# A two-block transformer kernel whose residual stream is held with the features on the partitions from the first stage to the last

## What is computed

```python
for n in range(4):
    x = x + 0.5 * swiglu(rms_norm(x, g), w_gate, w_up, w_down)    # d_ff 2816
    x = x + mixer[n](rms_norm(x, g))
    x = x + 0.5 * swiglu(rms_norm(x, g), w_gate, w_up, w_down)
# rms_norm(x, g) = x * rsqrt(mean(x * x, axis=-1) + 1e-6) * g
# swiglu(h, wg, wu, wd) = (silu(h @ wg) * (h @ wu)) @ wd
```

## Time and profile before

| | us |
|---|---|
| median of 3 runs | 2869.38 (2861.89 to 2871.81) |
| span of the profiled execution, first to last instruction | 2865.5 |
| TensorE busy | 2586.2 (90%) |
| VectorE busy | 1564.4 (55%) |
| ScalarE busy | 1133.1 (40%) |
| GpSimd busy | 88.5 (3%) |
| moved by DMA | 409.58 MB, 143 GB/s on average |

### The profile page before, as it was taken

How to read it: one execution, slowest core, us unless ns; L and a number is a source line. 1 busy time by engine, 2 the same in 40 slices (tenths; PEclk the granted TensorE clock), 3 DMA queues, 4 the chain that set the end, 5 groups by cost and what they waited for, 6 DMA issues and landing times.

```text
span 2865.5 us, 41213 instructions
## 1 busy us (share of the span) xinstructions
PE 2586.2 (90%) x17302; PEld 2356.7 (82%) x17302; DVE 1564.4 (55%) x1965; ACT 1133.1 (40%) x1254; POOL 88.5 (3%) x85
## 2 busy tenths in 40 slices
PE   5999977999999668999999888799999998887999
PEld 4998965899998547998999876689989897675898
DVE  3555664555555775455555644655555555456544
ACT  3333443433434244334334552343333345433432
POOL 2000000000000203000000000030000000000000
PEclk9999977999999779999999987999999999889999
DMA  5554521455455304554554422255545544222454
GB/s 167 187 190 133 177 74 33 158 190 179 160 190 162 115 0 106 189 190 157 181 189 151 135 90 69 89 164 188 186 154 189 167 150 130 85 89 74 162 184 138
DMA packets 306697, 409.58 MB, mean 143 GB/s; under 512 B 9367, under 2 KB 272861, under 8 KB 306589
## 3 DMA queue, kind: packets, MB, share of 16 engines
q1 hardware_dynamic: 303360, 400.61, 43.5%
q0 software_dynamic: 2496, 5.49, 1.1%
q10 hardware_dynamic: 732, 1.98, 0.2%
HBM read 407.00 MB, written 1.05 MB: 142 GB/s over the span
## 4 chain that ended last, share of the span: by engine, by line
PE 79%; DVE 12%; ACT 6%; issue 2%; DMA 1%; DVEq 0%; ACTq 0%; SPq 0%
PE bank L458 35%; PE acc L466 21%; PE bank L781 13%; ACT parts L393 3%; PE bank L723 2%; DVE parts L400 2%; PE bank L777 2%; PE bank L852 1%; DMA raw<-in_ffn_w_up 1%; PE bank L1721 1%; PE bank L871 1%; PE bank L639 1%; PE bank L1599 1%; DVE x L560 1%; DVE stat L613 1%
## 5 line engine op out<-in xcount | busy, mean ns | idle before, releaser
L400 DVE TENSOR_TENSOR parts<-raw,parts 128x2048 fp32r<-128x2048 f32 x383 | 877.9, 2292 | 927.1 <-ACT parts L393 923.3
L393 ACT ACTIVATE parts<-raw 128x2048 fp32r<-128x2048 f32 x383 | 730.6, 1908 | 1297.2 <-PE bank L458 630.4
L458 PEld LDWEIGHTS bank<-hT,parts 128*128 128x128 f32 x8448 | 1024.4, 192 | 9.2 <-DVE parts L400 2.5
L458 PE MATMUL bank<-hT,parts 128*128 128x256 f32 x8448 | 1028.2, 283 | 2.1 <-DVE parts L400 2.1
L466 PE MATMUL acc<-parts,gated 128*128 128x512 f32 x2400 | 564.8, 392 | 12.3 <-DVE gated L707 7.4
L466 PEld LDWEIGHTS acc<-parts,gated 128*128 128x128 f32 x2400 | 447.9, 189 | 104.3 <-issue 8.7
L781 PE MATMUL bank<-parts,hT 128*128 128x256 f32 (+2 forms) x3504 | 438.1, 288 | 15.3 <-DVE parts L400 9.9
L781 PEld LDWEIGHTS bank<-parts,hT 128*128 128x128 f32 x3504 | 433.3, 197 | 22.1 <-DVE parts L400 14.5
L528 DVE TENSOR_TENSOR silu_gate<-bank,silu_gate 128x512 f32<-128x512 f32 x88 | 60.9, 691 | 138.9 <-PE bank L458 138.9
L723 PE MATMUL bank<-squares,x 128*128 128x128 f32 x384 | 76.7, 380 | 58.7 <-DVE squares L752 52.9
L723 PEld LDWEIGHTS bank<-squares,x 128*128 128x128 f32 x384 | 71.4, 286 | 66.6 <-DVE squares L752 57.8
(11 more groups left out here) (342 smaller groups left out, 1528.9 us busy)
## 6 DMA issues: line engine op xcount, KB each, us to landing
raw<-in_ffn_w SPq DMA_DIRECT2D x132, 1024.0 KB, 5.2
raw<-in_w_in SPq DMA_DIRECT2D x52, 1024.0 KB, 5.3
raw<-in_ffn_w_gate SPq DMA_DIRECT2D x44, 1024.0 KB, 5.3
raw<-in_ffn_w_up SPq DMA_DIRECT2D x44, 1024.0 KB, 5.3
raw<-in_ffn_w_down SPq DMA_DIRECT2D x44, 1024.0 KB, 4.8
raw<-in_hy_w_in SPq DMA_DIRECT2D x22, 1024.0 KB, 5.3
raw<-in_hy_w_out SPq DMA_DIRECT2D x8, 1024.0 KB, 4.8
raw<-in_w_out SPq DMA_DIRECT2D x8, 1024.0 KB, 4.9
```

The costliest lines, as they stand in the source:

```text
L393: t.e.activation(parts[:, n % PARTS, 0, 0:size], raw[:, n % RAW, 0:size], ACT.Copy).then_inc(hi_ready, 1)
L400: t.e.tensor_tensor(parts[:, n % PARTS, 1, 0:size], raw[:, n % RAW, 0:size], parts[:, n % PARTS, 0, 0:size].bitcast(F32), ALU.subtract).th ...
L458: mm = pe.matmul(bank[:, up_bank(t, c, which), f * S:(f + 1) * S], slot_cols(s, w)[:, k, f * P:(f + 1) * P], hT[:, h, k, :], start=(k == 0 ...
```

## The change

The residual is kept as `xT`, eight tiles of 128 features by 256 tokens.

- Down and output products (`down_tile`, L486 of the new file) have the weights stationary and 256 tokens streaming: 48 matmuls of 256 columns for a piece in place of 24 of 512. Their sums come out with the features on the partitions, two feature tiles to a bank of `acc`, one bank after another in the last piece.
- `add_vector` adds each bank to `xT`; `hT` is `xT` times the gain, split, without the root and without a transpose. The squares of `xT` are summed over the eight tiles (`tensor_reduce`, L682); a matmul with a column of ones sums over the partitions (`root_col_tensor`); VectorE makes the root for each token; `root_row_tensor` spreads it over the partitions as `root_row`.
- Since `hT` lacks the root, every product of it is multiplied by the root as it leaves PSUM: token-major results by ScalarE with a scale per partition (two halves, since a half has its own column), feature-major ones by VectorE with `root_row`.
- The gates of the triple mixers and `mix` are feature-major too; their evacuation moves from ScalarE to VectorE, the sigmoid stays on ScalarE and works in SBUF. The transposes of `mix` are gone.
- At the start `x` is transposed once (16 transposes), at the end the result is transposed back and leaves in four transfers.

```diff
-        def down_product(pe, stationary, s, k, a, first, last):
+        def down_tile(pe, rows_hl, moving, d, first, last):
+
             for g, w in PASSES:
-                for n in range(2):
-                    mm = pe.matmul(acc[:, 2 * a + n, :], stationary(g), slot_rows(s, w)[:, k, n * 512:(n + 1) * 512],
-                                   start=(first and g + w == 0), stop=(last and g == 1), skip_group_check=True)
+                mm = pe.matmul(acc[:, d // 2, (d % 2) * S:(d % 2 + 1) * S], rows_hl(w)[:, d * P:(d + 1) * P], moving(g),
+                               start=(first and d % 2 == 0 and g + w == 0), stop=(last and g == 1),
+                               skip_group_check=True)
             return mm
 
-        def ffn_down(pe, c, s, last=False):
-            for a, f in [(a, f) for a in range(TT) for f in range(2)]:
-                mm = down_product(pe, lambda g: gated[:, g, c % 2, f * S + a * P:f * S + (a + 1) * P], s, f, a,
-                                  False, last and f == 1)
-                if last and (a, f) == (0, 1):
+        def ffn_down(pe, c, s, first=False, last=False):
+            for d in range(KD):
+                for f in range(2):
+                    mm = down_tile(pe, lambda w: slot_rows(s, w)[:, f, :],
+                                   lambda g: gated[:, g, c % 2, f * S:(f + 1) * S], d, first and f == 0, last and f == 1)
+                if last and d in (1, 3, 5):
                     mm.then_inc(acc_full, 1)
             mm.then_inc(piece_done, 1)
...
-            for b in range(4):
-                pe.matmul(acc[:, b, :], zeros[:, :], zeros[:, :].unsqueeze(1).to_broadcast([P, 4, P]), start=True,
-                          stop=False, skip_group_check=True)
+            all_taken(t)
             ffn_up(t, 0, arrived(t), 0, hT_waits(t))
-            ffn_up(t, 0, arrived(t), 1)
+            ffn_up(t, 0, arrived(t), 1, between=lambda: root_col_tensor(t))
+            root_row_tensor(t)
...
+                split_hi(t, n + PARTS, i)
+                if c == 0:
+                    t.see(root_col_ready)
+                    root_row_scalar(t)
+                act.wait_ge(gate_scaled, later(CHUNKS * k + c + 1, i, 2))
+                v = silu_gate[:, c % 2, :]
+                act.activation(v, v, ACT.Silu).then_inc(silu_ready, 1)
+                split_hi(t, n + PARTS + 1, i)
...
-                split_lo(t, n + 2, i)
+                if c == 0:
+                    root_col_vector(t)
+                    split_lo(t, n + PARTS)
+                    dve.wait_ge(root_row_ready, t.see(root_row_ready))
+                dve.wait_ge(piece_done, later(PARTS + n + 1, i, LOOP))
+                v = silu_gate[:, c % 2, :]
+                v2 = v.rearrange("p (f s) -> p f s", f=2)
+                dve.tensor_tensor(v2, halves(up_bank(t, c, 0)), root_rows(2), ALU.mult).then_inc(gate_scaled, 1)
+                if c:
+                    split_lo(t, n + PARTS, i)
                 dve.wait_ge(piece_done, later(PARTS + n + 2, i, LOOP))
+                dve.tensor_tensor(up_rows[:, :].rearrange("p (f s) -> p f s", f=2), halves(up_bank(t, c, 1)),
+                                  root_rows(2), ALU.mult).then_inc(gate_made, 1)
+                dve.wait_ge(gate_made, later(3 * (CHUNKS * k + c) + 1, i, 6))
                 dve.wait_ge(silu_ready, later(CHUNKS * k + c + 1, i, 2))
-                v = silu_gate[:, c % 2, :]
-                dve.tensor_tensor(v, bank_of(up_bank(t, c, 1)), v, ALU.mult).then_inc(gate_made, 1)
-                dve.wait_ge(gate_made, later(2 * (CHUNKS * k + c) + 1, i, 4))
+                dve.tensor_tensor(v, up_rows[:, :], v, ALU.mult).then_inc(gate_made, 1)
+                dve.wait_ge(gate_made, later(3 * (CHUNKS * k + c) + 2, i, 6))
                 dve.tensor_copy(gated[:, 0, c % 2, :], v).then_inc(gate_made, 1)
-                dve.wait_ge(gate_made, later(2 * (CHUNKS * k + c) + 2, i, 4))
+                dve.wait_ge(gate_made, later(3 * (CHUNKS * k + c) + 3, i, 6))
                 dve.tensor_tensor(gated[:, 1, c % 2, :], v, gated[:, 0, c % 2, :].bitcast(F32), ALU.subtract)\
                     .then_inc(gated_ready, 1)
-                split_lo(t, n + 3, i)
+                split_lo(t, n + PARTS + 1, i)
...
+        def root_col_tensor(t):
+
+            pe = t.e
+            pe.wait_ge(sums_ready, t.see(sums_ready))
+            for a in range(TT):
+                mm = pe.matmul(acc[:, 0, a:a + 1], sums[:, a * P:(a + 1) * P], one_col[:, :], start=True, stop=True)
+            mm.then_inc(sums_full, 1)
+
+        def root_row_tensor(t):
+
+            pe = t.e
+            pe.wait_ge(root_col_ready, t.see(root_col_ready))
+            for a in range(TT):
+                mm = pe.matmul(acc[:, 1, a * P:(a + 1) * P], root_col[:, a:a + 1].to_broadcast([P, P]), ident,
+                               start=True, stop=True)
+            mm.then_inc(root_row_full, 1)
+            t.roots += 1
+
+        def pre_scalar(t, at):
+
+            act = t.e
+            for b in range(4):
+                act.wait_ge(x_ready, t.see(x_ready))
+                for k in (2 * b, 2 * b + 1):
+                    act.activation(hT[:, 0, k, :], xT[:, k, :], ACT.Copy, scale=gain[:, at + k:at + k + 1])\
+                        .then_inc(hT_hi, 1)
+            act.activation(squares[:, :], xT[:, :, :].rearrange("p k s -> p (k s)"), ACT.Square).then_inc(x_squares, 1)
+            if t.piece:
+                next_hi(t)
...
+        def root_row_scalar(t):
+
+            act = t.e
+            act.wait_ge(root_row_full, t.see(root_row_full))
+            act.activation(root_row[:, :], acc[:, 1, 0:S], ACT.Copy).then_inc(root_row_ready, 1)
+            act.wait_ge(root_row_ready, t.see(root_row_ready))
...
+        def add_vector(t, b, scale):
...
+            acc_filled(t, b, scale is None)
+            v = xT[:, 2 * b:2 * b + 2, :]
+            if scale is None:
+                ins = dve.tensor_copy(v, acc_pair(b))
+            else:
+                ins = dve.scalar_tensor_tensor(v, acc_pair(b), scale, v, ALU.mult, ALU.add)
+            ins.then_inc(x_ready, 1)
...
+        def pre_vector(t, at, scale):
+
+            dve = t.e
+
+            def add(b):
+                add_vector(t, b, scale)
+
+            def low(b):
+                dve.wait_ge(hT_hi, t.see(hT_hi, 2))
+                for k in (2 * b, 2 * b + 1):
+                    dve.scalar_tensor_tensor(hT[:, 1, k, :], xT[:, k, :], gain[:, at + k:at + k + 1],
+                                             hT[:, 0, k, :].bitcast(F32), ALU.mult, ALU.subtract).then_inc(hT_ready, 1)
+
+            add(0)
+            for b in range(1, 4):
+                add(b)
+                low(b - 1)
+            low(3)
+            dve.wait_ge(x_squares, t.see(x_squares))
+            dve.tensor_reduce(sums[:, :], squares[:, :].rearrange("p (k s) -> p s k", k=KD), AX.X, ALU.add)\
+                .then_inc(sums_ready, 1)
+            if t.piece:
+                next_lo(t)
+
+        def root_col_vector(t):
+
+            dve = t.e
+            dve.wait_ge(sums_full, t.see(sums_full))
+            t.link(dve.tensor_copy(stat[:, 0, 0:TT], acc[:, 0, 0:TT]))
+            y, w = root_vector(t, stat[:, 0, 0:TT], D, last_factor=True)
+            dve.tensor_tensor(root_col[:, :], y, w, ALU.mult).then_inc(root_col_ready, 1)
...
-        def project_scalar(t, dsts, scale=1.0, func=ACT.Copy):
+        def project_scalar(t, dsts, func=ACT.Copy):
...
                 next_hi(t)
                 t.e.wait_ge(piece_done, through(t))
-                t.e.activation(dst, halves(b, dst.shape[-1]), func, scale=scale).then_inc(taken[b], 1)
+                for a in range(TT):
+                    ins = t.e.activation(dst[:, a, :], halves(b, dst.shape[-1])[:, a, :], func,
+                                         scale=root_col[:, a:a + 1])
...
         def gate_quarter(t, n):
-            project_scalar(t, [gt[:, :, n * COLS:(n + 1) * COLS]], func=ACT.Sigmoid)
+            project_rows_scalar(t, 1)
+            t.e.wait_ge(mix_gated, t.see(mix_gated))
+            v = gt[:, 2 * n:2 * n + 2, :]
+            t.e.activation(v, v, ACT.Sigmoid).then_inc(gates_ready, 1)
+
+        def gate_rows_vector(t, n):
+            project_rows_vector(t, [gt[:, 2 * n:2 * n + 2, :]])
+            t.e.sem_inc(mix_gated, 1)
 
         def gate_vector(t):
...
-            for a in range(TT):
-                if a:
-                    dve.wait_ge(piece_done, PARTS + t.piece + 1)
-                t.link(dve.tensor_tensor(dst[:, a, :], acc2()[:, a, :], gt[:, a, :], ALU.mult))
+            dve.wait_ge(gates_ready, t.see(gates_ready, 4))
+            for b in range(4):
+                acc_filled(t, b)
+                g, m = gt[:, 2 * b:2 * b + 2, :], mix[:, 2 * b:2 * b + 2, :]
+                t.done(dve.tensor_tensor(g if n else m, acc_pair(b), g, ALU.mult), acc_taken)
                 if n:
```

(10 more changed lines are left out.)

321 lines of the change are left out of this document (171 added, 150 removed).

## The result

| | before | after |
|---|---|---|
| median | 2867.12 us (4 runs) | 2992.67 us (4 runs, 2986.52 to 2999.59) |
| ratio | | 1.0436, 95% interval 1.041 to 1.0463 |
| span of the profiled execution | 2865.5 us | 2994.5 us |
| TensorE busy | 2586.2 us | 2635.7 us |
| mean granted clock | 0.939 | 0.920 |

A forecast was written before the change was run, and what follows sets the result against it. TensorE, busy for 90% of the span, was taken as the bound, so only its queue or waits ending last in it count. Terms summed to +45.4 us: 2865.5 + 45.4 + 3.9 = 2915 us, range 2868 to 2950.

The forecast's parts named there:

- Term 1: Down and output products: a piece takes 5.76 us in place of 5.46, +35.3 us over 120 pieces.
- The chunks' cover: FFN chunks: VectorE's added operation stays hidden, about 0.6 us of slack left; cover gone by 0.3 us would cost 26.
- rival 3: Down products at nearly the same rate per column in both forms, +7 instead of +35: 2887 us, chance 0.03.
- Term 2: Boundaries before an FFN: weight matmuls start before the root is ready, gaining 3.3 us at each of 7, -23.1 us.
- rival 1: Strided sum over eight tiles takes twice as long, 2.3 us more at each of 12 boundaries: 2941 us, chance 0.14.
- GpSimd: Its bias additions slow VectorE at two FFN boundaries, behind the sparse and first triple mixers: 3 us each, +6.
- Term 3: Other boundaries: hybrid mixer -3.1 us, sparse -0.5, triple mixers 2 x -3.0, start -2.3, end +1.
- Term 4: Triple mixers: gate emptying behind VectorE's split, neighbourhood attention +12.4 us, GLA +14.2, MLA +11; untransposed `mix` -3.5.
- The clock: Two gaps per boundary instead of one lower the granted clock: 0.4 us at each of 11, +4 (0 to +18).
- the faster one: Rival 4: VectorE's row does not end last at boundaries, and term 4's waits go: 2829 us, chance 0.11.
- the one with hidden waits: Rival 2: term 4's waits lie beside other work and the clock holds: 2873 us, chance 0.12.

The follow-up runs named there:

- bias_later: Changed kernel with the signal for GpSimd's bias additions given behind the first chunk of FFN 3 and 5, not before their boundary; 2983.92 us, ratio 1.0407.
- evac_first: Changed kernel with VectorE emptying a feature-major bank before it splits the next weight piece but one, not after; 2942.17 us, ratio 1.0263.
- split_first: Changed kernel with the next weight piece split before the squares and their sum at each boundary; 2943.81 us, ratio 1.0264.
- keep_busy: Changed kernel with eight matmuls of zeros at each of four places of the neighbourhood attention where TensorE waits; 2973.23 us, ratio 1.0377.
- both_orders: Changed kernel with the two orders of evac_first and split_first together; 2890.06 us, ratio 1.0097.

## Why the prediction was wrong

The sign was right and the size was not: +45 forecast, +125.5 measured, outside the range. The steps that failed are above all the price of the low clock (+4 forecast, +49.4 found), then the sum over eight tiles (2.29 us taken from a row without a stride, 3.84 measured), and the waits of terms 2 to 4 that hang on the order of VectorE's work. Step by step:

1. **Term 1, the products**: right. 5.76 us a piece as forecast, +35 forecast, +31 (21 to 41) measured by itself. The chunks' cover held. The +7 that the prediction estimated from the table in the Trainium skill (TensorE: Matmul & The Clock Gate, Back-to-back issue gap) isn't what these products cost; the row of the up step gave it. That settles rival 3.
2. **Term 2, the boundaries**: the mechanism and the order were right, two sizes in the sum weren't. N starts at T + 0.8 (0.7 forecast), N + 1 at T + 12.2 (10.9), N + 2 at T + 21.7 (19.2), so 0.7 us were gained, not 3.3. The failed terms are the sum at 2.29 us, which took 3.84, and N + 1 at full speed, whose first half took 4.4 us instead of 2.9. Before the first triple mixer N + 2 starts at T + 22.4 (1564.40 - 1542.03), where 18.6 was forecast and 21.6 stood before, so term 3's 3.0 us weren't gained there either. I had rival 1 for the first size (at 0.14, with 2.3 us): it came true at 1.5 us a boundary. The remark on 16-byte lines in the Trainium skill (SBUF — State Buffer, Door 1: The DMA port swizzle) pointed the right way, and the traces agree in direction, on VectorE's reading (3.83 us against 2.29) and on ScalarE's writing (4.13 against 1.90); I gave the row that reads without a stride more weight than it could bear.
3. **GpSimd**: 6 forecast for two boundaries. The two FFNs lie 20.1 - 2 x 3.4 = 13.3 us above what FFN 1, 2, 4 and 6 lost on the mean. I charged it on long operations, as in the earlier trace rows; it fell on the twelve small ones, and adds about the same 1 us to a step of 0.16 us as to one of 0.69. bias_later, where those steps are free of it, takes FFN 5 7.4 us down.
4. **Term 3**: the hybrid mixer was to change by -0.8 (its 8 pieces and -3.1) and changed by +6.6, the sparse by +0.7 and +4.3. The failed term in the hybrid is the emptying behind the split, +2.4 forecast; evac_first, which undoes it, gains 7.6 there. The sparse mixer goes to -0.5 with split_first, so its loss lies at the boundary.
5. **Term 4, the triple mixers**: the places were right, each was dearer. In the neighbourhood attention 16.6 us against 6.2: TensorE stands still 6.4 us longer, as priced, and the low clock takes 11.0 more (busy time beside that fell by 0.9). GLA, from the end of the down products ahead of it to the start of its own, lost 8.9 us against 7.1, of which the low clock has 0.9; no run takes it apart. The flips of MLA waited 8.2 us longer, 4.9 forecast: the two gates' emptying and the one more split between the keys' sum and the flips cost 3.9, but I didn't count that the sum for the keys' norm already starts 2.7 us behind the start of the fourth gate piece (1874.69 - 1872.01), where it was level with it before, or that this piece ran 1.5 us faster than before, which lengthens the wait behind it. The output projection came 1.4 us earlier, 1.74 forecast. The projections behind the boundary lost 4.8 us in a stretch that I took for untouched:

```profile
1568.00:1574.00 6.00, 6.00 (x30) 6.00 (x30) 0.62 (x1) 0.96 (x1) 0.00 (x0) 0.50 0.71 230
...
1580.00:1586.00 6.00, 6.00 (x53) 6.00 (x52) 3.03 (x3) 2.64 (x3) 0.00 (x0) 1.00 0.34 117
```

At clock 0.50 TensorE got through 30 matmuls in 6 us, at 1.00 through 53 (of the 30, 24 are the narrower ones of 96 columns; before, the same piece had 56 matmuls in 6 us, from 1533 to 1539, at 1.00).

6. **The clock**: +4 forecast, +49.4 found, and this is the largest single miss. I took 0.4 us for each of 11 boundaries and nothing in the mixers. It fell elsewhere: in FFN 1, 2, 4 and 6 the low clock takes 1.5 us less than before, since it had been low behind the old, longer wait too (granted 0.69 on the mean between T and T + 10.9), and 37.4 of the 49.4 us lie in the triple mixers. keep_busy shows the cause for the gate steps. In split_first the wait ahead of N + 1 and the low clock within it go together. For the stretch of step 5 the cause stays open: in both_orders, where N + 1 waits for nothing but 0.54 us in its middle, the granted clock is 0.50 from 1535 to 1541 all the same, and the 432 matmuls take 56.45 us, in the changed kernel 56.42.

By stages the 84 us missed are 47 in the triple mixers, 14 in FFN 3 and 5, 15 in the other FFNs, 11 in the other mixers, less the 4 forecast for the clock.

The rivals: the faster one and the one with hidden waits were wrong for the reason given with them: VectorE's row ended last at every boundary shown, and the waits of term 4 were waits. What I didn't see is that the loss hung on the *order* in which VectorE does the new work. The prediction took that order from the code as it stood and never asked what another order would give; with it turned round (both_orders) the kernel takes 2890 us, 25 under the forecast.

## What to carry to other kernels

When an operation moves to an engine that also does long ones (a weight split of 2.3 us), its price is the long one ahead of it, not its own 0.7 us: put the short operation for which another engine waits first. Price each new wait twice, once for itself and once for the clock behind it: here 80 us of waits came with 49 us of slowed work (22 us of that shown by keep_busy to hang on the waits), and filling four of the waits in each triple mixer with useless matmuls made the kernel faster. A layout that saves transposes pays only if the reductions across it are cheap: a strided sum cost 1.7 times one in a row, and moving the stride to the writer cost 2.23 us to save 1.54.

## What was not expected of the hardware

- A VectorE sum over elements 1024 bytes apart took 3.83 us for 2048 elements, one in a row 2.29; ScalarE's squares written 32 bytes apart took 4.13 us, in a row 1.90.
- With GpSimd adding in SBUF, VectorE's steps on 2 elements took 1.1 us instead of 0.16, about every second one.
- Eight bf16 matmuls of zeros (1.9 us) in a wait of 2.5 us kept the granted clock up (1.00, against 0.77 in the changed kernel); the piece behind took 6.0 us instead of 7.5.
- 16 matmuls that load 128 columns and stream 2 took 1.7 us, 0.11 each, little less than the 0.120 of one that streams 256.
